# The second block's banded attention: float32r scores in two products with stacked query parts, one bias table, and small operations once per four heads

## The reference, cut to what matters

```
s = einsum(q, k) * Dh ** -0.5                       # (group, head, 128 queries, 384 keys)
s = where(|dist| <= 128 and key exists, s - slope_h * |dist|, -inf)
m = max(max(s), sink_h)
p = exp(s - m)
o = (p / (sum(p) + exp(sink_h - m))) @ v
slope_h = 2 ** (-8 (h + 1) / 16)
```

## Time and profile before

| | |
|---|---|
| median of 3 runs | 3427.03 us |
| the three runs | 3340.12, 3427.03, 3492.56 us |
| span of the profiled execution, first to last instruction | 3498.2 us |
| busy in it | PE 85%, DVE 43%, ACT 28%, POOL 6% |
| mean granted TensorE clock | 0.854 of full |
| stage "w2" in it | 1469.1 to 1902.5 us |

### The profile page before, as it was taken

How to read it: one execution, slowest core, us unless ns; L and a number is a source line. 1 busy time by engine, 2 the same in 40 slices (tenths; PEclk the granted TensorE clock), 3 DMA queues, 4 the chain that set the end, 5 groups by cost and what they waited for, 6 DMA issues and landing times. The chain is left out here.

```text
span 3498.2 us, 37554 instructions
## 1 busy us (share of the span) xinstructions
PE 2989.8 (85%) x13760; PEld 2374.7 (68%) x13760; DVE 1504.5 (43%) x3662; ACT 972.0 (28%) x2200; POOL 196.1 (6%) x203
## 2 busy tenths in 40 slices
PE   3999957999565939899999998896696699999996
PEld 3888846779454728766666885772584588887875
DVE  3111367667888131244444114558413341424244
ACT  2121242446543121232222123450311321212121
POOL 1000020000200010000000000226000000000000
PEclk8999865999797969855555999699798799999998
DMA  2121200000001221000000120001213111111113
GB/s 83 49 73 50 86 1 1 1 1 2 1 1 48 97 74 50 19 7 13 7 13 34 49 73 28 1 1 54 82 49 118 43 48 49 49 49 46 50 47 117
DMA packets 91655, 144.86 MB, mean 41 GB/s; under 512 B 34256, under 2 KB 40528, under 8 KB 91472
## 3 DMA queue, kind: packets, MB, share of 16 engines
q1 hardware_dynamic: 84304, 117.28, 11.0%
q0 software_dynamic: 4864, 16.78, 1.2%
q10 hardware_dynamic: 2304, 8.39, 0.6%
HBM read 117.25 MB, written 25.17 MB: 41 GB/s over the span
## 5 line engine op out<-in xcount | busy, mean ns | idle before, releaser
L368 PE MATMUL banks<-h3T,mlwhi 128*128 128x512 f32 x1024 | 318.4, 392 | 9.4 <-DVE mlwlo L334 6.1
L368 PE MATMUL banks<-mlwhi,fT 128*128 128x512 f32 x1024 | 316.1, 390 | 3.3 <-ACT relu L2140 3.3
L368 PE MATMUL banks<-g1whi,hT 128*128 128x512 f32 (+1 forms) x1024 | 302.0, 378 | 5.7 <-DVE g1wlo L334 5.7
L334 DVE TENSOR_TENSOR mlwlo<-mlraw,mlwhi 128x512 fp32r<-128x512 f32 x128 | 87.7, 691 | 464.4 <-ACT mlwhi L311 464.4
L368 PEld LDWEIGHTS banks<-h3T,mlwhi 128*128 128x128 f32 x1024 | 192.9, 189 | 52.6 <-DVE mlwlo L334 6.5
L311 ACT ACTIVATE mlwhi<-mlraw 128x512 fp32r<-128x512 f32 x128 | 80.8, 632 | 526.9 <-PE banks L368 522.6
L368 PEld LDWEIGHTS banks<-mlwhi,fT 128*128 128x128 f32 x1024 | 191.6, 188 | 45.7 <-ACT relu L2140 6.3
L368 PEld LDWEIGHTS banks<-g1whi,hT 128*128 128x128 f32 x1024 | 189.2, 189 | 41.3 <-DVE g1wlo L334 6.1
L1053 PE MATMUL banks<-k2T,q2T 64*128 64x384 f32 (+1 forms) x256 | 194.1, 870 | 9.7 <-PEq L1495 9.7
L368 PE MATMUL banks<-h3T,mlwlo 128*128 128x512 f32 x512 | 200.1, 391 | 0.0
L368 PE MATMUL banks<-mlwlo,fT 128*128 128x512 f32 x512 | 199.2, 389 | 0.0
(11 more groups left out here) (448 smaller groups left out, 5760.2 us busy)
## 6 DMA issues: line engine op xcount, KB each, us to landing
mlraw<-in_w_up SPq DMA_DIRECT2D x64, 256.0 KB, 2.8
mlraw<-in_w_down SPq DMA_DIRECT2D x64, 256.0 KB, 2.7
g1raw<-in_w_in SPq DMA_DIRECT2D x56, 256.0 KB, 2.6
g3raw<-in_w_in SPq DMA_DIRECT2D x40, 256.0 KB, 2.6
g4raw<-in_w_out SPq DMA_DIRECT2D x32, 256.0 KB, 2.6
xt<-in_x SPq DMA_DIRECT2D x8, 512.0 KB, 6.6
z_scratch<-zst POOLq DMA_DIRECT2D x16, 256.0 KB, 2.6
cw<-in_cmp_w SPq DMA_DIRECT2D x2, 2048.0 KB, 9.2
```

The costliest lines, as they stand in the source:

```text
L334: nc.vector.tensor_tensor(wlo[n % RING][:, w_slice(n)], raw[n % RAW][:, w_slice(n)], f32(whi[n % RING][:, w_slice(n)]), ALU.subtract).then ...
L368: last = nc.tensor.matmul(out, l, r, start=(k == 0 and i == 0), stop=(k == job.nk - 1 and i == 2))
```

## The change

The second block's attention leaves `attention_stage` and gets a stage of its own, `window2_stage`.

- Scores: the query block is stacked on 128 partitions, the float32r part in one half and the float32r rest in the other, and multiplied by a float32r part of the keys and by their rest (the keys stand in both halves). These are two float32r products of 128 rows in place of one float32 product of 64 rows. ACT makes the first part for a block of queries (two activations of 64x1024), POOL the rest (two subtractions of 64x1024). The keys' two parts come out of the projection: ACT writes the first, DVE the rest, for all eight accumulators.
- Bias: the queries are scaled by 0.125 / slope in the projection, so one table of |dist| serves all heads; the slope is a constant in the fused DVE operation, which now writes the negated, scaled score and takes the minimum, so nothing has to be negated after it; ACT multiplies by -1. The sixteen-part table becomes one copy. 16 small memsets on DVE, in a block of their own before the projection, write the scales.
- Small operations: the sink's exponential, the sum, the reciprocal and the scaling into `yt` are done once for four heads. Values are multiplied by the 64 columns that are needed and four heads share a PSUM bank.
- DVE's order: bias and maximum of unit u+4 come first, then, for odd u, the copy of unit u-2, then, for every fourth u, an output.

```diff
-    tab = mem.at("wtab", kb, [P, ATT_HEADS, n], F32)
+    tab = mem.at("wtab", kb, [P, n], F32)
+    nsink = mem.at("wnsink", kb + 1.5, [P, ATT_HEADS], F32)
...
+            nc.vector.tensor_scalar(nsink[:], C["sink"][:], -1.0, None, ALU.mult).then_inc(dve_s, 1)
             dve.wait_ge(pool_s, 3)
-            for h in range(ATT_HEADS):
-                nc.vector.tensor_scalar(tab[:, h, :], base[:], 2.0 ** (-8.0 * (h + 1) / ATT_HEADS), None,
-                                        ALU.mult).then_inc(dve_s, 1)
-    return tab
+            nc.vector.tensor_copy(tab[:], base[:]).then_inc(dve_s, 1)
+    return tab, nsink
...
+def window2_stage(nc, sem, mem, ident, qT, k_hi, k_lo, v2, tab, nsink, q_kb, x_kb, pt_kb, st_kb, yt, y_free, psum,
+                  store):
+    X, AHEAD, LAG = 6, 4, 2
...
+            def scores(u):
+                t, h = divmod(u, ATT_HEADS)
...
+                if h == 0:
+                    pe.wait_ge(q_lo, 2 * (t + 1))
+                if u >= 4:
+                    pe.wait_ge(m_ready, u - 3)
+                out = psum[u % 4][:, 0:width(u)]
+                nc.tensor.matmul(out, qs[t % 2][:, h, :], k_hi[:, h // 4, cols], start=True, stop=False)
+                nc.tensor.matmul(out, qs[t % 2][:, h, :], k_lo[:, h // 4, cols], start=False, stop=True)\
+                    .then_inc(s_ready, 1)
+
+            def transposes(u):
+                pe.wait_ge(e_ready, u + 1)
+                if u >= 2:
+                    pe.wait_ge(dev if u % 2 else aev, u // 2)
...
+            def values(u):
+                t, h = divmod(u, ATT_HEADS)
+                k0, k1 = keys(u)
+                pe.wait_ge(dev if u % 2 else aev, u // 2 + 1)
+                if h % 4 == 0 and u >= 8:
+                    pe.wait_ge(o_done, u // 4 - 1)
...
+            for u in range(NU):
+                if u + AHEAD < NU:
+                    scores(u + AHEAD)
+                transposes(u)
+                if u >= LAG:
+                    values(u - LAG)
...
+        @block.scalar
...
+            for u in range(NU):
+                t, h = divmod(u, ATT_HEADS)
+                if h == 4 and t + 1 < NT:
+                    queries_hi(t + 1)
+                act.wait_ge(m_ready, u + 1)
+                nc.scalar.activation(x[u % X][:, 0:width(u)], x[u % X][:, 0:width(u)], ACT.Exp, scale=-1.0,
+                                     bias=low[:, t, h:h + 1], accum_out=tot[:, t, h:h + 1]).then_inc(e_ready, 1)
+                if h % 4 == 3:
+                    act.wait_ge(d_ready, u // 4 + 1)
+                    nc.scalar.activation(sk[:, t, 1, h - 3:h + 1], sk[:, t, 0, h - 3:h + 1], ACT.Exp)\
+                        .then_inc(k_ready, 1)
+                if u >= 2 and u % 2 == 0:
+                    evacuate(u - 2)
...
+        @block.gpsimd
+        def _(pool):
+            for t in range(NT):
+                pool.wait_ge(q_hi, 2 * t + 2)
+                for h in range(2):
+                    nc.gpsimd.tensor_tensor(qs[t % 2][half(h, 1), h:ATT_HEADS:2, :], qT[half(h), :, t * P:(t + 1) * P],
+                                            f32(qs[t % 2][half(h), h:ATT_HEADS:2, :]), ALU.subtract).then_inc(q_lo, 1)
...
+        @block.vector
...
+            def bias_max(u):
...
+                if h % 4 == 3:
+                    dve.wait_ge(m_ready, u + 1)
+                    nc.vector.tensor_tensor(sk[:, t, 0, h - 3:h + 1], low[:, t, h - 3:h + 1], nsink[:, h - 3:h + 1],
+                                            ALU.subtract).then_inc(d_ready, 1)
...
+            for u in range(NU):
+                if u + AHEAD < NU:
+                    bias_max(u + AHEAD)
+                if u >= 2 and u % 2 == 1:
+                    evacuate(u - 2)
+                if u >= 7 and u % 4 == 3:
+                    output(u // 4 - 1)
```

More of the change, by code:

```diff
@@ L1484, in _, with window2_tables @@
             nc.vector.tensor_copy(C["trinegr"][:], C["trineg"][:]).then_inc(dve_s, 1)
-def window2_tables(nc, sem, mem, kb, tmp_kb):
+def window2_tables(nc, sem, mem, C, kb, tmp_kb):
     n = 3 * P
-    tab = mem.at("wtab", kb, [P, ATT_HEADS, n], F32)
+    tab = mem.at("wtab", kb, [P, n], F32)
+    nsink = mem.at("wnsink", kb + 1.5, [P, ATT_HEADS], F32)
     ramp = mem.at("wramp", tmp_kb, [P, n], I32)
@@ L1955, in second_block, with _, q_place, q_job @@
     qT = mem.at("q2T", 0, [P, ATT_HEADS // 2, SEQ], F32)
-    kT = mem.at("k2T", 32, [P, ATT_KV, SEQ], F32)
-    v2 = mem.at("v2", 48, [P, NT, ATT_KV * HD], F32)
+    kT = [mem.at("k2T", 32 + 16 * i, [P, ATT_KV, SEQ], F32R) for i in range(2)]
+    v2 = mem.at("v2", 64, [P, NT, ATT_KV * HD], F32)
     dt_raw = mem.at("dt_raw", 184, [P, NT, 2 * SSM_HEADS], F32)
-    def cols_job(dst, j0, col, scale, wv=None):
+    qscale = mem.at("qscale", 183, [P, ATT_HEADS // 2], F32)
+    qsc = sem("qscale")
+    with nc.Block() as block:
+        @block.vector
+        def _(dve):
+            for j in range(ATT_HEADS // 2):
+                nc.vector.memset(qscale[0:64, j:j + 1], 0.125 / slope2(2 * j)).then_inc(qsc, 1)
+                nc.vector.memset(qscale[64:128, j:j + 1], 0.125 / slope2(2 * j + 1)).then_inc(qsc, 1)
+    def q_place(acc, j0):
+        return qT[:, j0 + acc // 2, (acc % 2) * 512:(acc % 2 + 1) * 512]
+    def q_job(j0, col):
+        return Job(hT, KT, [(w_view(w, col, 512), 0)], 512, False,
+                   act=Take(lambda e, ch, acc, ps, _: nc.scalar.activation(
+                       q_place(acc, j0), ps[:, :], ACT.Copy, scale=qscale[:, j0 + acc // 2:j0 + acc // 2 + 1]), even),
+                   dve=Take(lambda e, ch, acc, ps, _: nc.vector.tensor_scalar(
+                       q_place(acc, j0), ps[:, :], qscale[:, j0 + acc // 2:j0 + acc // 2 + 1], None, ALU.mult), odd),
+                   frees=lambda acc: "act" if even(acc) else "dve")
+    def k_place(i, acc):
+        return kT[i][:, acc // 2, (acc % 2) * 512:(acc % 2 + 1) * 512]
+    def k_lo(e, ch, acc, ps, _):
+        return nc.vector.tensor_tensor(k_place(1, acc), ps[:, :], f32(k_place(0, acc)), ALU.subtract)
+    def cols_job(dst, j0, col, scale):
         def place(acc):
             return dst(j0 + acc // 2)[:, (acc % 2) * 512:(acc % 2 + 1) * 512]
-        return Job(hT, KT, wv or [(w_view(w, col, 512), 0)], 512, False,
+        return Job(hT, KT, [(w_view(w, col, 512), 0)], 512, False,
                    act=Take(lambda e, ch, acc, ps, _: nc.scalar.activation(place(acc), ps[:, :], ACT.Copy, scale=scale),
@@ L1978, in second_block, with y_free @@
     gemm_stage(nc, sem, "g2", mem, 153,
-               [cols_job(lambda j: qT[:, j, :], 0, C_Q, 0.125), cols_job(lambda j: qT[:, j, :], 4, C_Q + 512, 0.125),
-                cols_job(lambda j: kT[:, j, :], 0, None, 1.0, k_views),
+               [q_job(0, C_Q), q_job(4, C_Q + 512),
+                Job(hT, KT, k_views, 512, False,
+                    act=Take(lambda e, ch, acc, ps, _: nc.scalar.activation(k_place(0, acc), ps[:, :], ACT.Copy)),
+                    dve=Take(k_lo), frees=lambda acc: "dve"),
                 Job(hT, KT, [(w_view(w, C_V, 256), 0), (w_view(w, C_DT, 32), 256)], 288, True, act=Take(v_act),
                     frees=lambda t: "act")], psum)
-    tab = window2_tables(nc, sem, mem, 56, 153)
-    yt = [mem.at("yt", 171 + 4 * i, [P, DM], F32) for i in range(2)]
+    tab, nsink = window2_tables(nc, sem, mem, C, 171, 153)
+    yt = [mem.at("yt", 174 + 4 * i, [P, DM], F32) for i in range(2)]
     y_st = [sem(f"y_st{i}") for i in range(2)]
[L1987 to L2001, removed]
+    def y_free(dve, t, g):
+        if g == 0 and t >= 2:
+            dve.wait_ge(y_st[t % 2], 16 * (t // 2))
     def store(sp, o_done):
         for t in range(NT):
-            sp.wait_ge(o_done, ATT_HEADS * (t + 1))
+            sp.wait_ge(o_done, ATT_HEADS // 4 * (t + 1))
             sp.dma_start(scr_y[t * P:(t + 1) * P, :], yt[t % 2][:]).then_inc(y_st[t % 2], 16)
@@ L2008, in store @@
             sp.wait_ge(y_st[i], 16 * NT // 2)
-    attention_stage(nc, sem, "w2", mem, C, units, 1, [big[:, 0:1024], big[:, 1024:2048]], psum, 80, 153, 167,
-                    store=store, width=3 * P, slots=6, ahead=4, lag=2)
+    window2_stage(nc, sem, mem, C["ident"], qT, kT[0], kT[1], v2, tab, nsink, 72, 153, 162, 168, yt, y_free, psum, store)
     xraw = mem.at("xraw", 0, [P, XBC_TILES, SEQ + 4], F32)
```

97 lines of the change are left out of this document (added).

## The result

| | before | after |
|---|---|---|
| runs beside each other, median | 3459.8 us (3340.12, 3427.03, 3492.56, 3498.71) | 3432.24 us (3430.44 to 3433.6) |
| profiled execution, its span | 3498.2 us | 3431.9 us |
| stage "w2" in the profile | 433 us at clock 0.50 | 366 us at clock 0.59 |

The kernel before has short executions (3328 to 3383 us over all sessions) and long ones (3491 to 3503 us), with two in between, and the comparison takes the shortest. Against 3340.12 us the changed kernel is slower by 2.6% (ratio 1.026, interval 1.024 to 1.029); against a long execution of 3495 us it is 1.8% faster. I had predicted 3340 us and a gain. The time came 92 us above that and 7 us above the range.

What follows compares the result with a forecast made beforehand. PE was taken to bound "w2" at half clock. The sum 3498.2 - 433.5 + 262 + 12 + 6 - 4 + 2 = 3343 us as a span, stated as 3340; forecast 3305 to 3365 (0.60), range 3235 to 3425.

Steps and rivals of the forecast that it cites:

- the clock: PE's clock in the new stage: 1.00 despite the new waits, save the first block of queries, 12 us.
- rival 4: Clock falls back for part of the stage, 20 to 80 us more, total 3365 to 3440; chance 0.07.
- Rival 1: PE's waits keep the clock at 0.50: stage 390 us, total 3459, or 3494 if values stay dear; chance 0.13.
- Rival 2: DVE's copy is done ahead of need, no wait, PE alone counts: total 3247 us; chance 0.10.
- Rival 3: Subtract from the median, not the profile, as the timings' difference may lie outside "w2": 3269 us; chance 0.10.
- The wait itself: In odd passes PE's transposes wait about 1.4 us for DVE's copy, which stands behind the current scores' bias.
- The chain's two sizes of the stage: New stage's length from its pairs of units with the wait: 262 us at clock 1.00, 390 at 0.50.
- Scores, transposes, values: PE's work per unit of 384 keys without waits: 1.40 us at clock 1.00, 2.49 at 0.50.
- The start: PE's first scores wait for ACT's two activations and POOL's two subtractions: 6 us; later query blocks hidden.
- The small terms: One table copy in place of 16 saves 4 us; the 16 memsets before the projection cost 2 us.
- the projection's zero: DVE and ACT handling eight key accumulators instead of four in the projection: covered, 0 us, up to 3 if not.
- The transposes: The skill's rule that transposes don't engage the full clock would suggest 0.50; kept as reason for a rival, not the sum.

Runs made afterwards that it cites:

- kernel 2: The changed kernel with DVE's copy of unit u-2 put ahead of the bias of unit u+4; median 3252.02 us.
- kernel 9: The changed kernel with DVE's copy a pass earlier (unit u-1 for even u, ahead of the bias of unit u+4); median 3238.85 us.
- kernels 4 and 5: The changed kernel with four, then eight unused float32r products on PE between scores and transposes in every odd pass; medians 3364.3 and 3347.17 us.
- Kernel 8: The kernel before with a burst of 32 dense unused products on PE at unit 24 of "w2"; six executions of 3337.82 to 3357.96 us.
- kernel 10: kernel 9 with the first query block's two subtractions moved from POOL to DVE; median 3235.85 us.
- kernel 7: The kernel before with 24 dense unused products on PE ahead of the first scores of "w2"; 3501.36, 3497.11, 3367.42 and 3504.33 us.

## Why the prediction was wrong

**The step that failed** is the clock: "Will it stay up with the new waits? ... I take clock 1.00". It stayed for 30 us and then was 0.50 for most of the stage, mean 0.59. Kernels 2 and 9 (hardly a wait, clock 0.97 and 0.96 over the stage) and 4 and 5 (the wait filled, clock 0.83 and 0.94) show that the wait is the cause: it is the one thing that they take away or cover, with the stage's own products unchanged. One support was the sentence "what kept it down were the 64-row float32 scores, and these go". Kernel 8 refutes it: the same scores ran at 1.00 for 175 us. The other was a stage with waits at 1.00, "di" in the earlier trace rows, and its busy share. The share was the wrong thing to compare: after had 18.0 of 29 us busy at 1.00 and 70.2 of 88 at 0.50. A slow PE is busier in the same chain, so busy share says little of the clock. In "di" the trace of before even has single waits as long as after's, at clock 1.00:

```profile
1022.98 0.88 PE L1067 MATMUL banks<-ident,dix 128*128 128x128 f32 x6 [1.80 <-DVE dix L1148]
```

So the length of a wait doesn't decide it by itself either. "di" has other products between its waits; why it holds and this stage doesn't wasn't tested.

**The rivals.** What happened is rival 4, the clock falls back for part of the stage, to which I gave 0.07, near its upper end (3440). Rival 1's mechanism is the same, with nothing held. Both together had 0.20, too little for a sum in which the clock decides over 128 us; and the range ended inside rival 4. Rival 2 (3247) turned out to be the time of the kernel without the wait, 3239 to 3252. Rival 3, to subtract from the median, falls: the distance between the executions of before fits the clock in "w2" (kernel 8), and where the wait is gone and the clock holds, the four executions of kernel 2 lie within 4 us of one another, those of kernel 9 within 7 and the six of kernel 10 within 16. That each long execution has its loss in "w2" was seen in three profiles; a short one of the unchanged kernel was never profiled.

**What I subtracted from.** The profiled execution was a long one, and I wrote that the difference "vanishes with the change". It does where the clock holds. But the sum of 3340 us was thereby no gain over a short execution of before, 3340.12 us. Even with the clock as I assumed it, the change would have gained nothing against that one.

**The wait itself** was right in place and size. Predicted: 2.89 us for an odd pass at 1.00, 3.98 at 0.50, pairs 4.29 and 6.47. Measured: 4.58 at 1.00 for a pair with the sink's difference (0.38 in it, forecast 0.15), and 6.64 at 0.50. PE's wait for DVE was 80 us in 60 pieces, 1.33 each, against "about 1.4"; none stood for ACT's copy. The chain's two sizes of the stage, 262 and 390 us, with the time at each clock (0.59 is 18% of the stage at 1.00), give 0.18 x 262 + 0.82 x 390 = 367 us; measured 366.

**Scores, transposes, values** at 1.00: forecast 1.40 us a unit, measured 1.35 where PE hardly waits (kernel 9), scores 0.44 (1559.92 to 1560.36). At 0.50: 2.49 forecast, 2.56 measured for an even unit. The wider estimate of rival 1, that values don't get cheaper for being 64 columns, falls.

**The start**: forecast 6 us between ACT's first activation and PE's first scores, measured 7.0:

```profile
1468.20 2.13 ACT L1622 ACTIVATE w2qs<-q2T 64x1024 fp32r<-64x1024 f32 x2 [4.12 <-PEq L1496]
1470.41 4.74 POOL L1652 TENSOR_TENSOR w2qs<-q2T,w2qs 64x1024 fp32r<-64x1024 f32 x2 [2.91 <-ACT w2qs L1622]
...
1475.21 0.58 PE L1574 MATMUL banks<-k2T,w2qs 128*128 128x256 f32 x1 [12.54 <-POOL w2qs L1652]
```

ACT is as forecast (1.07 each), POOL takes 2.37 each and not 1.96. The other seven blocks' parts were in time: that is PE's only wait for POOL.

**The small terms.** The table is one copy of 0.36 us in place of 4.39, 4 us less as forecast. The 16 memsets take 1296.76 to 1298.49 us, 1.8 with the last one, forecast 2. With the stage at 366 us the sum's other terms give 3498.2 - 433.5 + 366 + 2 - 4 = 3429, and the span is 3431.9: so the projection's zero is right to about 3 us.

**The transposes.** By the Trainium skill's rule that I weighed ("TensorE: Matmul & The Clock Gate", Part 4, transposes don't let the full clock engage) the low clock of after would be theirs. These runs speak against it: kernels 2 and 9 have the same 352 transposes among the same products and run at 1.00 but for the stage's ends. It would have given a low clock, but for a cause that these kernels rule out.

**What stays open:** what decides, in the kernel before, which level "w2" has in an execution; and whether the 1.20 us wait is what lost the lifted clock in kernel 7 while kernel 8, without a wait behind its burst, kept it to the last units (one profile each, so this is argued and not shown). Open too is what, besides the wait, makes this stage lose the clock where "di" keeps it.

## What to carry to other kernels

On an engine that works its list off in order, a copy that frees a buffer must not stand behind a step that waits for the same pass's product: here exchanging two lines of DVE's list was worth 180 us, 73 of them the wait itself and the rest TensorE's clock. When the bounding engine is at half its clock, or a change puts gaps between its products, work the sum out at both clocks, give both a real chance, and don't decide between them by a busy share from a stage with other products. And look at what the profiled execution is: if the timings lie 150 us apart, find the one of the profile's stages that can be that much shorter before you subtract from it.

## What the runs showed of the hardware

- The same stage of float32 products, without one wait on PE, ran at 0.50 for 433 us in one execution and, after a burst of 7.4 us, at 1.00 for 175 us in another. The 64-row float32 products don't force the low clock.
- Products whose results nobody reads raised the granted clock from 0.59 to 0.83 and 0.94 and took 68 and 85 us off the kernel.
- A DVE subtraction of 128x4 elements, 0.16 us in most passes, took 2.16 to 2.25 us in ten passes of kernels 4 and 5, each time while POOL's pair of 64x1024 subtractions ran.
- Two subtractions of 64x1024 elements with a float32r output took POOL 4.74 us and DVE 2.47 us:

```profile
1467.44 2.47 DVE L1695 TENSOR_TENSOR w2qs<-q2T,w2qs 64x1024 fp32r<-64x1024 f32 x2 [1.39 <-ACT w2qs L1622]
```
